# Sums of squares of queries and keys in the first attention: one matmul in full precision becomes two of parts

## The chip, the cores and the metric

The kernel runs on one core of a Trainium2 chip. The metric is the device time of one execution in microseconds (us). The core has TensorE (matmuls and the loads of their weights), VectorE, ScalarE and GpSimd, each with an instruction queue that it works through in order, and the queue that starts most transfers (SyncE).

## The reference

The kernel computes two transformer blocks one after the other, on 512 tokens of width 1024. The change lies in the first block's attention, which has 8 heads, each with two groups of 64 query and key columns:

```python
def rms_norm(x, g):
    xf = x.astype(jnp.float32)
    y = xf * lax.rsqrt(jnp.mean(xf * xf, axis=-1, keepdims=True) + EPS)
    return (y * g.astype(jnp.float32)).astype(x.dtype)

def diff_attention(q, k, v, q_norm_g, k_norm_g, ...):
    q = rms_norm(q, q_norm_g)
    k = rms_norm(k, k_norm_g)
    ...
        scores = jnp.einsum('bqhcd,bkhcd->bhcqk', q_blk, k).astype(jnp.float32) * scale
        scores = jnp.where(visible, scores, NEG_INF)
        probs = jax.nn.softmax(scores, axis=-1)
        diff = probs[:, :, 0] - lam * probs[:, :, 1]
```

What matters here is the mean of the squares of the 64 columns of each query and key. A second attention, an expert layer and two feed-forward layers follow; the change doesn't touch them.

## The kernel before

**Precision.** Most products are made of parts. An operand is split into a high part, a copy in the reduced 4-byte type (shown as fp32r), and a low part, the full value minus the high part, also stored in that type. `triple` (L719 to L721) issues three matmuls: high by high, high by low, low by high. ScalarE makes the high parts by `copy` (L1277), VectorE the low parts by `tt` with a subtraction (L1748). `linear` runs `triple` over k-steps of 128 rows: 8 k-steps of three matmuls are one projection to 128 columns for all 512 tokens. The sums of squares are different: one matmul of a constant matrix by the squares, both in plain 4-byte floats. The trace records such a matmul as two.

**Layout in the attention.** Features lie on the partitions and the 512 tokens on the columns. `bank[0]` to `bank[7]` are the eight banks of PSUM, where matmuls write. `qkf[i]` holds, for head h with i = h % 2, four buffers of 128 x 512: [0] and [1] for the query, [2] and [3] for the key; `qk[i]` is the same memory in the reduced type. In each pair the first is for the squares and later for the high part, the second for the raw values and later the scaled ones and the low part. `blk` is a constant 128 x 128 matrix with two blocks of ones, so that `blk` times the squares gives the sum over each group of 64, repeated on its partitions. `scr[6]` and `scr[7]` are the buffers for the roots of query and key.

**The order.** `attention_order` writes out one list of steps (235 of them), and every engine runs through the same list, doing its own part of each step. For a head from 2 to 6 the list from one query projection to the next scores of the head reads: q0 (k-steps 0 to 3 of the query projection), scores 4h-2, q1 (k-steps 4 to 7), qraw, turn 4h-3, weigh 4h-2, k0, scores 4h-1, k1, turn 4h-2, weigh 4h-1, v0, v1, vraw, scores 4h, oscale, turn 4h-1, weigh 4h, rows, scores 4h+1, g0, and so on. Each query block of a head is one step of scores, weigh (softmax and the difference of the two groups) and turn (transposing the weights through `tbank`). In short, by engine:

- TensorE. k1 (L845): waits for the square of the query, sums it into `bank[0]` (L846), then k-steps 4 to 7 of the key. v0 (L849): k-steps 0 and 1 of the value projection, waits for the square of the key, sums it into `bank[1]` (L854), then k-steps 2 to 4. v1: the sum of squares of the output of an earlier head into the same `bank[1]` (L862), which waits for the key's Ln to have read it, from head 2 on; then k-steps 5 to 7. Scores (L894, L896) of head h wait for the low part of its key. L908 are the transposes of turn.
- ScalarE. qraw: raw copy of the query out of `bank[0]`, then its square. k1: `root` of the query (Ln, then Exp, both at L1274), raw copy of the key, square. v0: a weight split, the query's high part, `root` of the key, the key's high part. Its other work between them: the exponentials of scores (two for each block), the high part of the turned weights (turn), and the high parts of weights (`whl<-raw`, 1024 columns).
- VectorE. k1: scales the query by the root (L1756). v0: low part of the query, scaling of the key, its low part. Its other work: the maxima of scores (L1913, L1914), weigh, the low part of the turned weights, and the low parts of weights.

A wait is an instruction on the engine that waits; what stands behind it in the queue waits as well. Weights are split four units ahead of their use. The constants land long before the attention.

Of the kernel before, what the change touches and what calls it, by code (L numbers as in the profile page):

```python
# [10 lines left out]
ALU = mybir.AluOpType  # L11
# [133 lines left out]
def f(ap):  # L145
    return ap.bitcast(F32)
# [345 lines left out]
def build(nc, a, out):  # L492
    with ExitStack() as ctx:
# [25 lines left out]
        scr_r, _ = at("scr_r", 10 * 512, F32R, offset=scr_off)  # L519
# [6 lines left out]
        rope_r, _ = at("rope_r", 1024, F32R, offset=rope_off)  # L526
# [7 lines left out]
        bank = [pb[:, 512 * i:512 * i + 512] for i in range(8)]  # L534
# [7 lines left out]
        def prm(name, i=0, n=1):  # L542
            return prm_t[:, PCOLS[name] + i:PCOLS[name] + i + n]

        ident, ones, blk, iota = cst(C_ID, 128), cst(C_ONE, 128), cst(C_BLK, 128), cst(C_IOTA, 128)
# [6 lines left out]
        Hh, Hl = cut(H_t, 8), cut(H_t[:, 4096:8192], 8)  # L552
# [19 lines left out]
        def wlo(j, o=0, n=None):  # L572
            return whi(j, 1024 + o, n or units[j][2])

        prod, act, dve, pool = signal("pe_products"), signal("act_results"), signal("dve_results"), signal("pool_results")
# [3 lines left out]
        cst_in, prm_in, lam_in = signal("constants_landed", 16), signal("parameters_landed", 16), signal("lambdas_landed", 16)  # L579
# [23 lines left out]
        qk = [cut(S_t[:, 8192 + 2048 * i:10240 + 2048 * i], 4) for i in range(2)]  # L603
        qkf = [cut(ST_t[:, 8192 + 2048 * i:10240 + 2048 * i], 4) for i in range(2)]
        vv = [cut(S_t[:, 12288 + 1024 * i:13312 + 1024 * i], 2) for i in range(2)]
        vvf = [cut(ST_t[:, 12288 + 1024 * i:13312 + 1024 * i], 2) for i in range(2)]
        dts = [cut(S_t[:, 14336 + 1024 * i:15360 + 1024 * i], 2) for i in range(2)]
        turned_hi = S_t[:, 14336:16000].rearrange("p (b q) -> p b q", b=13)
        turned_lo = (rope_r[:, 0:896].rearrange("p (b q) -> p b q", b=7),
                     S_t[:, 16000:16384].rearrange("p (b q) -> p b q", b=3))  # L610
        tbank, obank = bank[6], bank[7]
# [103 lines left out]
        def tensor(eng, e):  # L715
            q = Waits(eng, units)
# [6 lines left out]
            def linear(j, o, hh, hl, ready, done, ks=range(8), kk=8, n=T, start=True, stop=True):  # L723
                q.wait_ge(w_lo, j + 1)
                for k in ks:
                    q.wait_ge(dve, ready[k])
                    c = slice(128 * k, 128 * k + 128)
                    last = triple(o[:, 0:n], whi(j)[:, c], wlo(j)[:, c], hh[k], hl[k],
                                  start and k == 0, stop and k == kk - 1)
                if k == kk - 1:  # L730
                    last.then_inc(prod.up(("w", j), done), 1)
# [96 lines left out]
            def first_attention():  # L828
                for step in attention:
# [12 lines left out]
                        jk = q.unit("w_in", 8 + h)  # L842
                        linear(jk, bank[1], Hh, Hl, h1, None, range(4))
                    elif what == "k1":
                        q.wait_ge(act, ("q_sq", h))  # L845
                        e.matmul(bank[0], blk, qkf[h % 2][0], start=True, stop=True, skip_group_check=True).then_inc(  # L846
                            prod.up(("qs", h)), 1)
                        linear(jk, bank[1], Hh, Hl, h1, ("k", h), range(4, 8))
                    elif what == "v0":  # L849
                        jv = q.unit("w_in", 16 + h)  # L850
                        q.wait_ge(act, ("q_ln", h))
                        linear(jv, bank[0], Hh, Hl, h1, None, range(2))
                        q.wait_ge(act, ("k_sq", h))
                        e.matmul(bank[1], blk, qkf[h % 2][2], start=True, stop=True, skip_group_check=True).then_inc(  # L854
                            prod.up(("ks", h)), 1)
                        linear(jv, bank[0], Hh, Hl, h1, None, range(2, 5))
                    elif what == "v1":
                        before = ("k_ln", h)
                        for o in step[2]:
# [400 lines left out]
        def scalar(eng, e):  # L1260
# [11 lines left out]
            def run(func, o, x, own=False, **kw):  # L1272
                table(func, own)
                return e.activation(o, x, func, **kw)  # L1274

            def copy(o, x):
                return e.activation(o, x, ACT.Copy)  # L1277
# [127 lines left out]
            def first_attention():  # L1405
                for step in attention:
# [4 lines left out]
                    if what == "qraw":  # L1411
                        q.wait_ge(prod, ("q", h))
                        q.wait_ge(prod, ("scores", 4 * h - 5) if h > 1 else ("brr", 7))
                        copy(qkf[i][1], bank[0])
                        run(ACT.Square, qkf[i][0], bank[0]).then_inc(act.up(("q_sq", h)), 1)
                    elif what == "k1":
                        q.wait_ge(dve, ("q", h - 1) if h else ("m", 7))
                        root((("q_ln", h), ("q_r", h)), bank[0], scr[6], 64, ("qs", h))
                        q.wait_ge(prod, ("k", h))
                        copy(qkf[i][3], bank[1])  # L1420
                        run(ACT.Square, qkf[i][2], bank[1]).then_inc(act.up(("k_sq", h)), 1)
                    elif what == "v0":
                        q.wait_ge(dve, ("q_scaled", h))
                        copy(qk[i][0], qkf[i][1]).then_inc(act.up(("q_hi", h)), 1)
# [314 lines left out]
        def vector(eng, e):  # L1739
# [7 lines left out]
            def tt(o, x, y, op):  # L1747
                return e.tensor_tensor(o, x, y, op)  # L1748
# [6 lines left out]
            def stt(o, x, s, y, op0, op1, **kw):  # L1755
                return e.scalar_tensor_tensor(out=o, in0=x, scalar=s, in1=y, op0=op0, op1=op1, **kw)  # L1756
# [164 lines left out]
            def first_attention():  # L1921
                for step in attention:
                    what, h = step[0], step[1]
                    i = h % 2
                    if what in ("q0", "k0", "g0"):
                        weights("w_in", {"q0": 0, "k0": 8, "g0": 44}[what] + h)
                    if what == "k1":
                        q.wait_ge(act, ("q_r", h))
                        stt(qkf[i][1], qkf[i][1], prm("q_norm_g"), scr[6], ALU.mult, ALU.mult).then_inc(dve.up(("q_scaled", h)), 1)
                    elif what == "v0":  # L1930
                        q.wait_ge(act, ("q_hi", h))
                        tt(qk[i][1], qkf[i][1], f(qk[i][0]), ALU.subtract).then_inc(dve.up(("q", h)), 1)
# [847 lines left out]
```

## Time and profile before

| | |
|---|---|
| median of 3 runs | 2969.61 us (2969.41 to 2971.81) |
| profiled execution | 2972.36 us, span 2970.2 us |
| TensorE matmuls busy | 2921.5 us, 98% of the span |
| weight loads busy | 2509.6 us, 84% |
| VectorE busy | 1906.8 us, 64% |
| ScalarE busy | 1152.3 us, 39% |
| GpSimd busy | 842.9 us, 28% |
| chain that ended last | PE 80%, DVE 12%, ACT 4%, issue 3%, POOL 1% |
| first attention | about 250 to 527 us |

In the rows below PE is TensorE's matmuls, PEld its weight loads, DVE VectorE, ACT ScalarE. Matmuls are pipelined: one recorded with 0.39 us can have the next start 0.23 us after its own start. The duration of an instruction on DVE and ACT includes its latency; the next one on the same engine starts 0.06 to 0.13 us before that end if it doesn't need the result. The executed instruction's line is the helper's where a helper issues it (L1277 is every `copy`).

### The profile page before, as it was taken

What the parts mean: (1) busy time and instruction counts of PE and PEld (TensorE: products, weight loads), DVE (VectorE), ACT (ScalarE), POOL (GpSimd) and SP (SyncE); (2) the same over time, 40 slices, a digit from 0 to 9 for tenths busy, and PEclk for the clock granted to TensorE, in tenths of its full rate; (3) what the DMA queues carried; (4) which work ended last, traced back from release to release, by engine and by line L of the source; (5) the groups of instructions that cost most, each with busy time, mean ns of one, the idle gap of its engine ahead of it and who ended that gap; (6) DMA issues with size and microseconds to landing.
All of it is one profiled execution on the core that took longest, in us unless ns stands there. A gap on an engine that the chain in (4) does not pass through costs nothing.

```text
span 2970.2 us, 35823 instructions
## 1 busy us (share of the span) xinstructions
PE 2921.5 (98%) x14079; PEld 2509.6 (84%) x14079; DVE 1906.8 (64%) x3255; ACT 1152.3 (39%) x1704; POOL 842.9 (28%) x523
## 2 busy tenths in 40 slices
PE   8999999999999999999999999999999999999999
PEld 6877777789889999999999999998888877788887
DVE  6664665578888895426787788865444567644443
ACT  5674665443333334433323223223222355532221
POOL 0000000228788888872332232321000400210000
PEclk9999999999999999999999999999999999999999
DMA  4325564336656666798988888842332321133222
GB/s 141 112 92 212 199 223 167 132 103 144 136 127 139 153 154 146 166 272 322 333 311 308 287 310 314 318 142 86 99 100 94 122 71 50 51 99 99 93 93 71
DMA packets 240808, 489.29 MB, mean 165 GB/s; under 512 B 97664, under 2 KB 149440, under 8 KB 240128
## 3 DMA queue, kind: packets, MB, share of 16 engines
q1 hardware_dynamic: 175680, 417.87, 42.3%
q0 software_dynamic: 64960, 69.14, 10.3%
q8 instruction: 111, 1.82, 0.2%
q14 instruction: 57, 0.47, 0.0%
HBM read 443.18 MB, written 77.23 MB: 175 GB/s over the span
## 4 chain that ended last, share of the span: by engine, by line
PE 80%; DVE 12%; ACT 4%; issue 3%; POOL 1%; DMA 0%; SPq 0%; POOLq 0%; ACTq 0%
PE pb L719 25%; PE pb L721 25%; PE pb L720 25%; DVE whl L1748 2%; ACT scr L1274 2%; DVE ST L1748 1%; ACT whl L1277 1%; PE pb L1011 1%; DVE ST L1756 1%; DVE S L1748 1%; DVE su L1997 1%; DVE ST L1998 1%; DVE su L2000 1%; DVE scr L1748 1%; PE pb L894 1%
## 5 line engine op out<-in xcount | busy, mean ns | idle before, releaser
L719 PE MATMUL pb<-H,whl 128*128 128x512 f32 (+1 forms) x2400 | 939.7, 392 | 6.4 <-ACT scr L1274 2.3
L721 PE MATMUL pb<-H,whl 128*128 128x512 f32 (+1 forms) x2400 | 911.5, 380 | 0.0
L720 PE MATMUL pb<-H,whl 128*128 128x512 f32 (+1 forms) x2400 | 910.8, 380 | 0.0
L1748 DVE TENSOR_TENSOR whl<-raw,whl 128x1024 fp32r<-128x1024 f32 (+5 forms) x554 | 650.7, 1189 | 256.3 <-ACT whl L1277 219.8
L1277 ACT ACTIVATE whl<-raw 128x1024 fp32r<-128x1024 f32 (+5 forms) x554 | 544.6, 1003 | 361.2 <-PE pb L721 360.1
L719 PE MATMUL pb<-S,whl 128*128 128x448 f32 (+2 forms) x1732 | 654.9, 378 | 14.2 <-DVE S L1748 5.7
L720 PE MATMUL pb<-S,whl 128*128 128x448 f32 (+2 forms) x1732 | 649.6, 375 | 0.0
L721 PE MATMUL pb<-S,whl 128*128 128x448 f32 (+2 forms) x1732 | 649.5, 375 | 0.0
L719 PEld LDWEIGHTS pb<-H,whl 128*128 128x128 f32 x2400 | 451.4, 188 | 83.8 <-issue 8.8
L720 PEld LDWEIGHTS pb<-H,whl 128*128 128x128 f32 x2400 | 451.5, 188 | 72.2 <-issue 6.0
L721 PEld LDWEIGHTS pb<-H,whl 128*128 128x128 f32 x2400 | 450.6, 188 | 71.9
L2400 POOL DMA_INDIRECT gd<-scr,place x256 | 438.2, 1712 | 137.8 <-issue 77.1
L719 PEld LDWEIGHTS pb<-S,whl 128*128 128x128 f32 x1732 | 327.9, 189 | 60.9 <-DVE S L1748 7.2
L720 PEld LDWEIGHTS pb<-S,whl 128*128 128x128 f32 x1732 | 327.8, 189 | 42.6 <-issue 1.2
L721 PEld LDWEIGHTS pb<-S,whl 128*128 128x128 f32 x1732 | 327.6, 189 | 42.5
L2379 POOL TENSOR_TENSOR pad<-X 128x512 f32<-128x512 f32 x32 | 46.2, 1442 | 862.4 <-DVE X L1748 833.3
L1274 ACT ACTIVATE scr<-pb 128x448 f32<-128x448 f32 (+1 forms) x130 | 71.0, 546 | 386.2 <-PE pb L721 364.5
L1748 DVE TENSOR_TENSOR scr<-pb,scr 128x512 f32<-128x512 f32 x96 | 66.0, 691 | 210.7 <-PE pb L721 199.7
L2433 POOL DMA_INDIRECT scr<-in_pv_rows,su x64 | 94.8, 1482 | 232.1 <-DVE scr L1756 204.8
L1277 ACT ACTIVATE S<-GA 128x896 fp32r<-128x896 f32 x60 | 57.2, 953 | 252.6 <-DVE GA L1748 247.0
L2387 POOL DMA_INDIRECT scr<-in_pu_rows,su x64 | 91.8, 1434 | 217.0 <-DVE scr L1756 167.0
L1748 DVE TENSOR_TENSOR X<-X,pb 128x448 f32<-128x448 f32 (+1 forms) x144 | 86.2, 630 | 92.8 <-PE pb L721 78.8
(224 smaller groups left out, 2573.8 us busy)
## 6 DMA issues: line engine op xcount, KB each, us to landing
raw<-in_pu SPq DMA_DIRECT2D x128, 512.0 KB
raw<-in_pv SPq DMA_DIRECT2D x128, 512.0 KB
raw<-in_w_in SPq DMA_DIRECT2D x72, 512.0 KB
ad<-scr SPq DMA_DIRECT2D x128, 224.0 KB
GA<-gd SPq DMA_DIRECT2D x60, 448.0 KB, 4.2
GA<-ad SPq DMA_DIRECT2D x60, 448.0 KB, 5.9
raw<-in_wg SPq DMA_DIRECT2D x44, 512.0 KB
raw<-in_wu SPq DMA_DIRECT2D x44, 512.0 KB
```

Of the source, the lines that this page charges most:

```text
L719: e.matmul(o, lh, h, start=start, stop=False, skip_group_check=True)
L720: e.matmul(o, lh, l, start=False, stop=False, skip_group_check=True)
L721: return e.matmul(o, ll, h, start=False, stop=stop, skip_group_check=True)
L894: e.matmul(b[:, 0:keys], x[r, t], y[r, 0:keys], start=start, stop=False, skip_group_check=True)
L1011: last = e.matmul(bank[gbank[n % 4]][:, c], hot2[n % 4][:, c], hot1[n % 4][:, c], start=True, stop=True, skip_group_check=True)
L1274: return e.activation(o, x, func, **kw)
L1277: return e.activation(o, x, ACT.Copy)
L1748: return e.tensor_tensor(o, x, y, op)
L2379: e.tensor_tensor(one_sq if k else sum_sq, x, x, ALU.mult).then_inc(pool.up(), 1)
L2387: e.indirect_dma_start(urow[j % 3] if j < UROWS else tail_row[j % 4], None, a["pu_rows"], bass.IndirectOffsetOnAxis(ap=expert[:, j:j + 1], ...
L2400: e.indirect_dma_start(g_rows, bass.IndirectOffsetOnAxis(ap=place[:, b, h, k:k + 1], axis=0), TSv[:, b, h, k:k + 1], None, compute_op=ALU. ...
L2433: e.indirect_dma_start(tail_row[j % 4], None, a["pv_rows"], bass.IndirectOffsetOnAxis(ap=expert[:, j:j + 1], axis=0)).then_inc(row_in[j % ...
```

## The change

The matmul of `blk` with the squares becomes two, of `blk_r` with the high part and with the low part of the squares, into the same bank. `blk_r` is a copy of `blk` in the reduced type, made once by ScalarE in head 0, in a free part of `rope_r`. The high parts get buffers of their own, `sq_hi`, in the memory of `scr[6]` and `scr[7]`; the low parts go to `qk[i][0]` and `qk[i][2]`, over the squares. ScalarE's order in qraw and k1 is now: square, wait for it, high part, raw copy (before: raw copy, square). VectorE gets a subtraction in qraw, a step in which it had nothing to do, and one at the end of k1. TensorE waits in k1 and v0 for the raw copy and for the low part. In v0 the sum for the key stands behind three k-steps of the value projection, and two follow it (before: two and three).

```diff
+        blk_r, sq_hi = rope_r[:, 896:1024], [scr_r[:, 3072:3584], scr_r[:, 3584:4096]]
...
                     elif what == "k1":
-                        q.wait_ge(act, ("q_sq", h))
-                        e.matmul(bank[0], blk, qkf[h % 2][0], start=True, stop=True, skip_group_check=True).then_inc(
+                        q.wait_ge(act, ("q_raw", h))
+                        q.wait_ge(dve, ("q_sq_lo", h))
+                        e.matmul(bank[0], blk_r, sq_hi[0], start=True, stop=False, skip_group_check=True)
+                        e.matmul(bank[0], blk_r, qk[h % 2][0], start=False, stop=True, skip_group_check=True).then_inc(
                             prod.up(("qs", h)), 1)
                         linear(jk, bank[1], Hh, Hl, h1, ("k", h), range(4, 8))
                     elif what == "v0":
                         jv = q.unit("w_in", 16 + h)
                         q.wait_ge(act, ("q_ln", h))
-                        linear(jv, bank[0], Hh, Hl, h1, None, range(2))
-                        q.wait_ge(act, ("k_sq", h))
-                        e.matmul(bank[1], blk, qkf[h % 2][2], start=True, stop=True, skip_group_check=True).then_inc(
+                        linear(jv, bank[0], Hh, Hl, h1, None, range(3))
+                        q.wait_ge(act, ("k_raw", h))
+                        q.wait_ge(dve, ("k_sq_lo", h))
+                        e.matmul(bank[1], blk_r, sq_hi[1], start=True, stop=False, skip_group_check=True)
+                        e.matmul(bank[1], blk_r, qk[h % 2][2], start=False, stop=True, skip_group_check=True).then_inc(
                             prod.up(("ks", h)), 1)
-                        linear(jv, bank[0], Hh, Hl, h1, None, range(2, 5))
+                        linear(jv, bank[0], Hh, Hl, h1, None, range(3, 5))
...
                     if what == "qraw":
                         q.wait_ge(prod, ("q", h))
                         q.wait_ge(prod, ("scores", 4 * h - 5) if h > 1 else ("brr", 7))
-                        copy(qkf[i][1], bank[0])
                         run(ACT.Square, qkf[i][0], bank[0]).then_inc(act.up(("q_sq", h)), 1)
+                        if h == 0:
+                            q.wait_ge(cst_in, "cst")
+                            copy(blk_r, blk).then_inc(act.up("blk_r"), 1)
+                        q.wait_ge(act, ("q_sq", h))
+                        q.wait_ge(dve, ("q_scaled", h - 1) if h else ("m", 7))
+                        copy(sq_hi[0], qkf[i][0]).then_inc(act.up(("q_sq_hi", h)), 1)
+                        copy(qkf[i][1], bank[0]).then_inc(act.up(("q_raw", h)), 1)
                     elif what == "k1":
...
                         q.wait_ge(prod, ("k", h))
-                        copy(qkf[i][3], bank[1])
                         run(ACT.Square, qkf[i][2], bank[1]).then_inc(act.up(("k_sq", h)), 1)
+                        q.wait_ge(act, ("k_sq", h))
+                        if h:
+                            q.wait_ge(dve, ("k_scaled", h - 1))
+                        copy(sq_hi[1], qkf[i][2]).then_inc(act.up(("k_sq_hi", h)), 1)
+                        copy(qkf[i][3], bank[1]).then_inc(act.up(("k_raw", h)), 1)
...
-                    if what == "k1":
+                    if what == "qraw":
+                        q.wait_ge(act, ("q_sq_hi", h))
+                        tt(qk[i][0], qkf[i][0], f(sq_hi[0]), ALU.subtract).then_inc(dve.up(("q_sq_lo", h)), 1)
+                    elif what == "k1":
                         q.wait_ge(act, ("q_r", h))
                         stt(qkf[i][1], qkf[i][1], prm("q_norm_g"), scr[6], ALU.mult, ALU.mult).then_inc(dve.up(("q_scaled", h)), 1)
+                        q.wait_ge(act, ("k_sq_hi", h))
+                        tt(qk[i][2], qkf[i][2], f(sq_hi[1]), ALU.subtract).then_inc(dve.up(("k_sq_lo", h)), 1)
```

## Rows read from the trace of the kernel before

**Rows 1.** Busy time by stretch, one head: busy (x instructions), clock, DMA share.

```profile
394.00:426.00 32.00, 32.00 (x163) 24.09 (x164) 20.10 (x46) 19.63 (x43) 0.00 (x0) 1.00 0.56 206
```

**Rows 2.** Waits of the weight loads, 255 to 495 us: in total, times, longest.

```profile
PEld pb L854 <- ACT ST L1274: 3.1, 8, 0.4
PEld pb L894 <- DVE S L1748: 0.8, 2, 0.5
```

**Rows 3.** Order of time, TensorE, head 5: start, duration, engine, line, operation.

```profile
414.17 1.10 PE L846 MATMUL pb<-ST,cst 128*128 128x512 f32 x2
...
415.34 0.39 PE L720 MATMUL pb<-H,whl 128*128 128x512 f32 x1
...
419.43 0.39 PE L721 MATMUL pb<-H,whl 128*128 128x512 f32 x1
419.81 1.12 PE L854 MATMUL pb<-ST,cst 128*128 128x512 f32 x2
...
421.00 0.40 PE L720 MATMUL pb<-H,whl 128*128 128x512 f32 x1
...
422.84 1.02 PE L862 MATMUL pb<-ST,cst 128*128 128x512 f32 x2
...
423.93 0.40 PE L720 MATMUL pb<-H,whl 128*128 128x512 f32 x1
...
425.88 0.55 PE L894 MATMUL pb<-S 64*128 64x128 f32 x6
```

**Rows 4.** Order of time, ScalarE, head 5; idle time before in brackets.

```profile
410.33 0.60 ACT L1277 ACTIVATE ST<-pb 128x512 f32<-128x512 f32 x1 [0.34 <-PE pb L721]
410.82 0.59 ACT L1274 ACTIVATE ST<-pb 128x512 f32<-128x512 f32 x1
411.30 0.39 ACT L1277 ACTIVATE S<-pb 128x256 fp32r<-128x256 f32 x1
...
417.44 0.68 ACT L1274 ACTIVATE scr<-pb,cst 128x512 f32<-128x512 f32 x1
418.15 0.63 ACT L1274 ACTIVATE scr<-scr 128x512 f32<-128x512 f32 x1
...
419.17 0.59 ACT L1274 ACTIVATE ST<-pb 128x512 f32<-128x512 f32 x1
419.64 0.49 ACT L1277 ACTIVATE S<-pb 128x384 fp32r<-128x384 f32 x1
...
420.96 0.64 ACT L1277 ACTIVATE S<-ST 128x512 fp32r<-128x512 f32 x1
421.48 0.70 ACT L1274 ACTIVATE scr<-pb,cst 128x512 f32<-128x512 f32 x1
```

**Rows 5.** Order of time, VectorE, head 5.

```profile
411.72 0.42 DVE L1748 TENSOR_TENSOR rope_r<-pb,S 128x256 fp32r<-128x256 f32 x1 [3.00 <-ACT S L1277]
...
414.58 0.68 DVE L1913 TENSOR_REDUCE sm<-pb 128x1 f32<-128x512 f32 x1
...
422.29 0.68 DVE L1748 TENSOR_TENSOR S<-ST,S 128x512 fp32r<-128x512 f32 x1
...
424.33 0.69 DVE L1748 TENSOR_TENSOR S<-ST,S 128x512 fp32r<-128x512 f32 x1 [0.70 <-ACT S L1277]
```

**Rows 6.** Order of time, heads 0 and 1, VectorE, TensorE, weight loads.

```profile
268.08 0.69 DVE L1748 TENSOR_TENSOR S<-ST,S 128x512 fp32r<-128x512 f32 x1 [0.70 <-ACT S L1277]
...
269.10 0.55 PE L894 MATMUL pb<-S 64*128 64x128 f32 x6
...
298.15 0.41 PEld L894 LDWEIGHTS pb<-S 64*128 64x128 f32 x6 [0.47 <-DVE S L1748]
```

**Rows 7.** Order of time, TensorE, end of the stage.

```profile
527.82 0.51 PE L719 MATMUL pb<-S,whl 128*128 128x512 f32 x1 [1.53 <-DVE S L1748]
...
531.94 0.51 PE L719 MATMUL pb<-S,whl 128*128 128x512 f32 x1 [1.78 <-DVE scr L1748]
```

**Rows 8.** Busy time by stretch there: the clock is the last but two.

```profile
530.00:540.00 10.00, 8.21 (x29) 6.53 (x29) 6.74 (x9) 4.41 (x7) 0.00 (x0) 0.83 0.46 156
```

## The prediction

> **What bounds the kernel now.** I read the page first: TensorE is busy 98% of the span, so what it does without waiting is on the path. Then the busy time by stretch: in the 32 us of one head of the first attention TensorE is busy for all 32.00 us at a granted clock of 1.00, VectorE for 20.10 and ScalarE for 19.63 [rows 1]. So removed TensorE time counts in full here, and the other two engines have room on average. The average isn't enough, because all three engines follow one written-out order. The third view is the list of waits of the weight loads from 255 to 495 us: the key sum of squares, L854, waits for ScalarE in every head, 8 times of 0.4 us at most, 3.1 us in all, and the score matmuls L894 wait twice for the key's low part [rows 2]. Of each 0.4 us TensorE itself loses only 0.15 (419.43 + 0.23 = 419.66 to 419.81), since a prefetched load stands ahead of its matmul [rows 3]. Small as that is, it says that L854 has no slack. So the fourth view is the order of time of head 5, engine by engine [rows 3 to 5]; heads 2 to 7 have these rows six times, 31.9 us apart; one set stands for them. The reader is to find there what L854 waits for and how far back that chain goes without a gap.
>
> **The chain before L854.** ScalarE gets the query projection at 410.33, copies and squares it, and at 411.30 makes the high part of the turned weights [rows 4]. VectorE, idle for 3.00 us, starts on that at 411.72 and is then busy without a gap: low part, weighing, a weight split, the maxima of scores 19 at 414.58 [rows 5]. The scores themselves end at about 414.35 (L846 follows them at 414.17 while they drain) [rows 3], so the maxima wait for VectorE by 0.2 us. ScalarE's exponentials wait for the maxima, and behind them stand, in its order, the Ln and Exp of the query root (417.44, 418.15), copy and square of the key (the square at 419.17) [rows 4]; L854 starts at 419.81, 0.05 after the square ends at 419.76 [rows 3]. From 410.33 to 419.81 this is a chain of ScalarE and VectorE work; whatever is put into it comes out at L854.
>
> **What is removed.** A sum of squares in full precision is two recorded matmuls that hold TensorE for four passes. After L862, which nothing holds up, the next L720 starts at 423.93; one pass of 0.23 earlier is the end of the sum: 423.70 - 422.84 = 0.86. After L846 it is 415.34 - 0.23 - 414.17 = 0.94, after the waiting L854 421.00 - 0.23 - 419.81 = 0.96: a weight load that isn't prefetched shows with 0.10 [rows 3]. No row has a pass with the block matrix in the reduced type; the nearest are the passes of the projections, 0.23 apart with a new weight load each. I take 0.46 for two, 0.56 behind a wait. Bounds: nothing gained (0.94) and 0.46. So L846 gives back 0.38 us a head, and L854 with its wait (419.43 + 0.23 = 419.66 to 420.77, 1.11 us) up to 0.65.
>
> **What the query side adds.** The square comes first, then a copy to its high part, which waits for the finished square, then the raw copy. The wait costs 0.59 + 0.03 (the Exp starts 0.03 after the end of the Ln, 417.44 + 0.68 to 418.15) where the square's successor came after 0.48: 0.14. The added copy, SBUF to SBUF, has a pace of 0.52 (420.96 to 421.48) [rows 4]. Together 0.66. VectorE's new subtraction has the form of the one at 422.29, 0.68 us [rows 5]; it waits for the high part (411.58) and ends at 412.30. L846 at 414.17 is covered: 1.9 us of slack. But the high part of the turned weights moves from 411.30 to 411.96 and VectorE's next start from 411.72 to 412.38, and from there the chain has no gap: maxima 415.24, Ln 418.10, Exp 418.81. Queued behind VectorE's new wait are the turned weights, weighing and the split; none of these has a tight reader on TensorE but the maxima. I bound this shift by 0 (absorbed) and 0.80 (the copy at 0.63 in full); I take 0.66.
>
> **What the key side adds.** The same edit once more. Square 419.35 to 419.94; high part 419.97 to 420.60; VectorE's low part, behind the query scaling, which is done by 420.2, 420.63 to 421.31; TensorE 421.36 instead of 419.81. TensorE itself arrives at 419.66 - 0.38 + 3 x 0.23 (the third k-step now stands ahead) = 419.97, so it idles for 1.39 us: the moved step covers 0.69 of 2.1 us. It is not lost work, for it is then missing behind: two k-steps instead of three. Behind the key's square ScalarE is late by 2 x 0.66 = 1.32: turned weights 420.96, query high part 422.28, Ln of the key 422.80 to 423.50 [rows 4].
>
> **What is late next.** L862, the sum for the head output before, overwrites the bank that this Ln reads and waits for it. Before, the Ln ended at 422.18 and L862 started at 422.84: 0.66 of slack. Now TensorE arrives at 421.36 + 0.56 + 6 x 0.23 = 423.30 and the Ln ends at 423.50, so L862 starts at 423.55, with 0.10 for its load: +0.81 against 422.84. The passes up to L894 (425.88) are unchanged. The key's low part starts at 424.33 [rows 5]; 1.32 later it ends at 426.34, before L894 starts at 426.69. After L894 all three engines are late by the same 0.81, so the next head starts the same chain over: 0.81 x 6 for heads 2 to 7 = 4.9 us. The price of the passes drops out, since ScalarE sets the time.
>
> **Heads 0 and 1.** Head 1 has no L862, and its scores already wait for the key's low part (the weight loader idles 0.47 before 298.15) [rows 6]; the whole 1.32 shows: 1.3 us. In head 0 there are no weights to turn and no maxima, so only the key side counts: square after the key product, which TensorE now ends 0.40 earlier, two copies and the wait: the Ln comes 0.3 later, the key's low part ends at 269.05 instead of 268.77, and L894 stands at 269.10 [rows 6]: 0.0. The copy of the block matrix (128 columns) lies in ScalarE's idle time there. Bounds for head 0: -0.9 (both gains) to +0.3.
>
> **Sum.** 0 + 1.3 + 4.9 = 6.2 us more. The scores of head 7 carry it, and the chain to the end of the stage runs on from them through VectorE and ScalarE, so it is kept. The profiled execution took 2972.36 us (span 2970.2), 2.75 above the median of 2969.61. Against its own time: 2978.6; as a median 2975.8, or +0.21%. A measurement of this kernel tells about 0.2%, 5.9 us, from no change.
>
> **Rivals.** (A) The chain isn't as tight as I read it and the third k-step covers the key side: then L846 gives 0.38 and L854 0.65 in 8 heads, -8.2 us, 2961.4. It needs the key's parts within 0.16 us of where the square now ends (419.97 against 419.81); against it stand three operations in a row that take 1.9 us. It decides from 1.39 us: a chain shorter by that much leaves no stall. (B) The query side's shift is absorbed, as VectorE's 3.00 us of idle time before 411.72 suggests; against it, that idle time lies before, not behind. Then only 0.66 reaches the Ln: L862 at 422.89 plus the load, +0.15 x 6, and 0.66 in head 1: +1.6, 2971.2. (C) The clock. At 527.82 TensorE resumes after 1.53 us of idle time at full pace; at 531.94 it resumes after 1.78 more [rows 7], and in the stretch from 530 to 540 the granted clock is 0.83 on average, where it was 1.00 before [rows 8]: 0.17 x 10 us / 0.5 = 3.4 us at 1.2 instead of 2.4 GHz, 1.7 us of work lost. With a stall of 1.39 and one of 0.25 in each of seven heads, 7 x 1.7 on top: +18.1, 2987.7. For it speaks the likeness, against it that the second gap is small. The Trainium skill, "TensorE: Matmul & The Clock Gate", section "HAM oscillation — how this bites in real kernels", says that waits between bursts of matmuls bring the slow clock back; the trace agrees at 531.94 and doesn't at 527.82.
>
> **How the numbers follow.** Forecast 0.75, A 0.07, B 0.14, C 0.04. The forecast's own range has 0.5 to 1.1 us a head in heads 2 to 7 and 1.0 to 1.6 in head 1: +4.0 to +8.2, 2973.6 to 2977.8; the border of 5.9 us lies in its middle, so 0.41 of it is slower and 0.34 the same. With B and some room above: 2970.4 to 2979.5. Slower 0.41 + 0.04, the same 0.34 + 0.14, faster 0.07.
>
> **What would show it.** Right: L854 with an idle time of about 1.4 us behind VectorE in heads 1 to 7; the maxima of the last score block of a head 0.66 later against L846; L862 behind the key's Ln; heads 32.7 us apart instead of 31.9. Wrong: L854 follows the third k-step at once (A); the Ln of the query root isn't later against L846 (B); passes of 0.43 us inside the stage (C).

## The result, and the profile after

| | before | after |
|---|---|---|
| median | 2970.63 us (2969.41 to 2971.81, 9 runs) | 2976.66 us (2974.59 to 2983.99, 9 runs) |
| profiled execution | 2972.36 us, span 2970.2 | 2976.09 us, span 2974.3 |

The ratio is 1.0021, with a 95% interval of 1.0013 to 1.0029: 6.0 us slower in the median, and the interval reaches from 3.9 to 8.6 us. The forecast was 6.2 us.

The page: TensorE has 5.2 us less to do (2921.5 us before), and the span is longer all the same.

```profile
span 2974.3 us, 35872 instructions
...
PE 2916.3 (98%) x14079; PEld 2510.0 (84%) x14079; DVE 1917.4 (64%) x3271; ACT 1162.1 (39%) x1721; POOL 844.0 (28%) x523
```

The stretch of head 6 (the columns are those of [rows 1], where TensorE was busy for all 32.00 us). Now it is idle for 32.00 - 30.87 = 1.13 us, with its clock unchanged; VectorE has 0.55 us more in the same 32 us and ScalarE 0.42:

```profile
426.00:458.00 32.00, 30.87 (x159) 23.32 (x158) 20.65 (x45) 20.05 (x45) 0.00 (x0) 1.00 0.56 206
```

What the weight loads waited for from 255 to 500 us (in total, times, longest), against [rows 2]. The wait of the key's sum, here L858, has grown from 3.1 to 5.3 us; new are waits of L720, the value projection, for the query's Ln and of L867, the sum for the head before, for the key's Ln; the scores L899 wait in all eight heads. In heads 2 to 7 that is 0.35 us each and only the load that nothing prefetches: the scores start 0.33 us after the last pass of the value projection before (425.55 to 425.88) and 0.32 after (430.04 to 430.36). Heads 0 and 1 wait for the key's low part, 0.83 and 1.23 us:

```profile
PEld pb L720 <- ACT scr L1279: 7.7, 7, 1.1
...
PEld pb L858 <- ACT ST L1282: 5.3, 8, 0.7
...
PEld pb L899 <- DVE S L1763: 4.2, 8, 1.2
PEld pb L867 <- ACT scr L1279: 2.6, 6, 0.4
```

Head 5 in order of time, TensorE, against [rows 3] (L848 and L849 are the query's two passes, L858 and L859 the key's, L867 was L862, L899 was L894, L913, the transposes, was L908):

```profile
417.85 0.48 PE L848 MATMUL pb<-scr_r,rope_r 128*128 128x512 f32 x1
...
418.40 0.40 PE L720 MATMUL pb<-H,whl 128*128 128x512 f32 x1
...
421.16 0.49 PE L913 MATMUL pb<-cst,scr 128*128 128x128 f32 x3
422.50 0.50 PE L720 MATMUL pb<-H,whl 128*128 128x512 f32 x1 [0.85 <-ACT scr L1279]
...
425.14 0.47 PE L858 MATMUL pb<-scr_r,rope_r 128*128 128x512 f32 x1 [0.28 <-ACT S L1282]
...
425.69 0.39 PE L720 MATMUL pb<-H,whl 128*128 128x512 f32 x1
...
427.23 1.12 PE L867 MATMUL pb<-ST,cst 128*128 128x512 f32 x2
...
430.36 0.55 PE L899 MATMUL pb<-S 64*128 64x128 f32 x6
```

ScalarE, against [rows 4] (the square is L1279, copies are L1282):

```profile
414.00 0.60 ACT L1279 ACTIVATE ST<-pb 128x512 f32<-128x512 f32 x1 [0.34 <-PE pb L722]
414.63 0.63 ACT L1282 ACTIVATE scr_r<-ST 128x512 fp32r<-128x512 f32 x1
415.17 0.58 ACT L1282 ACTIVATE ST<-pb 128x512 f32<-128x512 f32 x1
415.64 0.38 ACT L1282 ACTIVATE S<-pb 128x256 fp32r<-128x256 f32 x1
...
421.76 0.68 ACT L1279 ACTIVATE scr<-pb,cst 128x512 f32<-128x512 f32 x1
...
423.02 0.58 ACT L1279 ACTIVATE ST<-pb 128x512 f32<-128x512 f32 x1
423.63 0.63 ACT L1282 ACTIVATE scr_r<-ST 128x512 fp32r<-128x512 f32 x1
424.17 0.58 ACT L1282 ACTIVATE ST<-pb 128x512 f32<-128x512 f32 x1
424.64 0.48 ACT L1282 ACTIVATE S<-pb 128x384 fp32r<-128x384 f32 x1
...
426.48 0.69 ACT L1279 ACTIVATE scr<-pb,cst 128x512 f32<-128x512 f32 x1
```

VectorE, against [rows 5] (L1763 at 415.29 and 424.30 are the two new low parts, at 416.05 the turned weights', L1928 the first of the maxima, 429.32 the key's low part):

```profile
415.29 0.69 DVE L1763 TENSOR_TENSOR S<-ST,scr_r 128x512 fp32r<-128x512 f32 x1 [2.90 <-ACT scr_r L1282]
416.05 0.42 DVE L1763 TENSOR_TENSOR rope_r<-pb,S 128x256 fp32r<-128x256 f32 x1
...
418.91 0.68 DVE L1928 TENSOR_REDUCE sm<-pb 128x1 f32<-128x512 f32 x1
...
424.30 0.69 DVE L1763 TENSOR_TENSOR S<-ST,scr_r 128x512 fp32r<-128x512 f32 x1 [0.40 <-ACT scr_r L1282]
...
429.32 0.69 DVE L1763 TENSOR_TENSOR S<-ST,S 128x512 fp32r<-128x512 f32 x1 [0.70 <-ACT S L1282]
```

The profile names ScalarE for the idle time ahead of L858. Of the two things that L858 waits for, the raw copy ended at 424.17 + 0.58 = 424.75 and VectorE's low part at 424.30 + 0.69 = 424.99, so the low part is the later.

The positions are best read from the start of the query's sum in each head:

| from the query's sum, heads 2 to 7 | before | forecast | after |
|---|---|---|---|
| maxima of the last scores start | 0.41 | 1.07 | 1.06 |
| key's sum starts | 5.64 | 7.19 | 7.29 |
| sum for the head before starts | 8.67 | 9.38 | 9.38 |
| scores start | 11.70 | 12.52 | 12.51 |
| (head 1) scores start | 10.92 | 12.24 | 12.23 |

From the start of head 0's sum of the query to score block 28 the kernel before takes 230.77 us, the changed one 236.69. The 5.92 us between them are the effect but for 0.08: from score block 28 to the last sum of squares of the stage it takes 33.43 us before and 33.51 after. I call the first distance the stage's and use it below, because it repeats to 0.02 us (236.67 in another execution), while the time of a whole execution varies by several us.

### The profile page after: what moved, and what is told of

The parts are those of the page before. It is cut to its first block, busy times and chain, and to the rows that moved or that the text cites. A ratio compares the mean times of both kernels' runs of the same rounds, so it can differ in the third digit from the quotient of the medians.

```text
span 2974.3 us, 35872 instructions
## 1 busy us (share of the span) xinstructions
PE 2916.3 (98%) x14079; PEld 2510.0 (84%) x14079; DVE 1917.4 (64%) x3271; ACT 1162.1 (39%) x1721; POOL 844.0 (28%) x523
## 4 chain that ended last, share of the span: by engine, by line
PE 78%; DVE 13%; ACT 6%; issue 2%; POOL 1%; DMA 0%; SPq 0%; POOLq 0%; ACTq 0%
PE pb L720 25%; PE pb L722 25%; PE pb L721 25%; DVE whl L1763 2%; ACT scr L1279 2%; ACT whl L1282 1%; DVE S L1763 1%; PE pb L1016 1%; DVE su L2017 1%; DVE ST L2018 1%; DVE su L2020 1%; DVE ST L1763 1%; DVE ST L1771 1%; DVE scr L1771 1%; DVE scr L1763 1%
## 5 line engine op out<-in xcount | busy, mean ns | idle before, releaser
L720 PE MATMUL pb<-H,whl 128*128 128x512 f32 (+1 forms) x2400 | 933.5, 389 | 12.2 <-ACT scr L1279 8.0
L1763 DVE TENSOR_TENSOR whl<-raw,whl 128x1024 fp32r<-128x1024 f32 (+5 forms) x554 | 650.4, 1188 | 247.2 <-ACT whl L1282 242.2
L1282 ACT ACTIVATE whl<-raw 128x1024 fp32r<-128x1024 f32 (+5 forms) x554 | 544.8, 1003 | 357.9 <-PE pb L722 356.7
L720 PE MATMUL pb<-S,whl 128*128 128x448 f32 (+2 forms) x1732 | 654.2, 378 | 15.6 <-DVE whl L1763 5.8
L720 PEld LDWEIGHTS pb<-H,whl 128*128 128x128 f32 x2400 | 451.9, 188 | 87.4 <-ACT scr L1279 11.2
L720 PEld LDWEIGHTS pb<-S,whl 128*128 128x128 f32 x1732 | 327.4, 189 | 62.5 <-DVE S L1763 7.1
L1279 ACT ACTIVATE scr<-pb 128x448 f32<-128x448 f32 (+1 forms) x130 | 70.9, 545 | 379.0 <-PE pb L722 350.8
L1763 DVE TENSOR_TENSOR scr<-pb,scr 128x512 f32<-128x512 f32 x96 | 66.0, 690 | 210.1 <-PE pb L722 199.1
L1282 ACT ACTIVATE S<-GA 128x896 fp32r<-128x896 f32 x60 | 57.2, 953 | 255.5 <-DVE GA L1763 255.5
L1763 DVE TENSOR_TENSOR X<-X,pb 128x448 f32<-128x448 f32 (+1 forms) x144 | 86.2, 629 | 89.0 <-PE pb L722 73.8
```

Source lines behind the costliest of these rows:

```text
L720: e.matmul(o, lh, h, start=start, stop=False, skip_group_check=True)
```

## The experiments

The distances are those of one execution each (those of a head are medians over heads 2 to 7). The ratio compares the times of 8 to 11 executions with those of the kernel before on the same chip, with a 95% interval.

| run | maxima | key's sum | head before's sum | scores | head 1 scores | stage | ratio of the times |
|---|---|---|---|---|---|---|---|
| before | 0.41 | 5.64 | 8.67 | 11.70 | 10.92 | 230.77 | |
| changed, again (e8) | 1.06 | 7.29 | 9.38 | 12.52 | 12.23 | 236.67 | 1.0019 (1.0009 to 1.0028) |
| e1 query alone | 1.06 | 6.30 | 9.34 | 12.38 | 11.57 | 235.04 | 1.0024 (1.0015 to 1.0034) |
| e2 key alone | 0.41 | 6.64 | 8.74 | 11.88 | 11.58 | 232.62 | 1.0009 (1.0000 to 1.0019) |
| e3 two k-steps ahead | 1.06 | 7.29 | 9.90 | 12.95 | 12.22 | 239.62 | 1.0030 (1.0019 to 1.0040) |
| e4 one split moved | 0.20 | 6.44 | 8.53 | 11.65 | 11.38 | 230.81 | 1.0005 (0.9995 to 1.0014) |
| e5 both splits moved | 0.20 | 6.44 | 8.37 | 11.38 | 11.36 | 233.43 | 1.0007 (0.9998 to 1.0016) |
| e6 before, splits moved | 0.20 | 5.44 | 8.46 | 11.50 | 10.70 | 229.88 | 0.9998 (0.9988 to 1.0007) |
| e7 key ahead of root | 0.20 | 5.98 | 7.83 | 11.51 | 11.51 | 234.96 | 1.0033 (1.0020 to 1.0047) |
| e9 reordered | 0.20 | 5.98 | 7.82 | 10.86 | 10.67 | 225.40 | 0.9991 (0.9982 to 1.0000) |
| e10 before, splits in idle time | 0.20 | 5.45 | 8.49 | 11.53 | 10.72 | 229.50 | 0.9998 (0.9989 to 1.0007) |
| e11 before, one copy more | 0.89 | 6.12 | 9.16 | 12.20 | 11.41 | 234.20 | 1.0013 (1.0004 to 1.0022) |

**Query alone, key alone (e1, e2).** The change taken apart. For the key, e1 goes back on ScalarE to the lines marked + here, and on TensorE and VectorE to those of the kernel before (left out); e2 does the same for the query:

```diff
-                        run(ACT.Square, qkf[i][2], bank[1]).then_inc(act.up(("k_sq", h)), 1)
-                        q.wait_ge(act, ("k_sq", h))
-                        if h:
-                            q.wait_ge(dve, ("k_scaled", h - 1))
-                        copy(sq_hi[1], qkf[i][2]).then_inc(act.up(("k_sq_hi", h)), 1)
-                        copy(qkf[i][3], bank[1]).then_inc(act.up(("k_raw", h)), 1)
+                        copy(qkf[i][3], bank[1])
+                        run(ACT.Square, qkf[i][2], bank[1]).then_inc(act.up(("k_sq", h)), 1)
...
```

> The change for the query alone, the key as in the kernel before. All offsets are from the start of the query's sum in head 5 (before: L846 at 414.17; L854 5.64 later, L862 8.67, L894 11.71). Theory (a chain from the query projection through turned weights, maxima, exponentials and roots sets the time): the chain is 0.66 us longer, so the key's sum comes at 6.30, L862 at 9.33, the scores at 12.37, although the query's sum holds TensorE 0.38 us less. 0.66 in each of heads 1 to 7, about -0.3 in head 0: score block 28 starts 4.3 us later than before, the time rises by about 4.3 us. Rival 1 (the passes are what counts and the chain has slack): -0.38 in each head, -3.0 us. Rival 2 (the loss comes from the key side alone): 0.

> The change for the key alone, the query as in the kernel before. Theory: the key's sum comes 6.52 after the start of the query's (before 5.64), the next head's sum L862 waits for the key's Ln (0.66 later, against 0.66 of slack) and comes at 8.82 (before 8.67), the scores 0.15 later; head 1, whose scores wait for the key's low part, 0.66, head 0 0.25: score block 28 starts 1.8 us later than before, the time rises by about 1.8 us. With the query alone this adds up to the 6.1 us of the whole change. Rival 1 (the key side carries the loss): 5 to 6 us. Rival 2 (passes count): -0.40 a head plus the wait of 0.15, -4.4 us.

Measured: 4.27 and 1.85 us more in the stage, 6.12 together against 5.92 for both. The larger loss comes from the half whose own sum was covered: the query's sum lost nothing at its own place, its extra ScalarE work came out at the key's sum 6 us later. The key's half is nearly absorbed by the 0.66 us of slack of the sum for the head before (8.74 against 8.67).

**One copy more (e11).** The chain by itself, without any pass changed:

```diff
                     if what == "qraw":
...
+                        q.wait_ge(dve, ("q_scaled", h - 1) if h else ("m", 7))
+                        copy(scr_r[:, 3072:3584], bank[0])
                         copy(qkf[i][1], bank[0])
```

> The kernel before the change with one copy more on ScalarE in qraw, out of the query's bank into memory that nobody reads, ahead of the raw copy. Theory: the copy has a pace of 0.49 us and all of it comes out at the key's sum, which TensorE has no slack for: 6.13 after the query's (5.64), the sum for the head before 9.16, the scores 12.19; 0.49 in heads 1 to 7, nothing in head 0: 3.4 us more, score block 28 234.2 us after head 0's sum of the query. Rival (ScalarE is busy 61% of this stage and hides it): 0.

3.43 us in the stage, 0.49 in each of seven heads, and the maxima are late by 0.48 already. A copy that nobody reads, on an engine that is idle for 12 of 32 us, costs its whole pace. It shows the chain of the prediction by itself.

**The moved k-step (e3).**

> The changed kernel with the key's sum behind two k-steps of the value projection, as before, in place of three. Theory: the sum starts at the same time (the parts come no earlier, TensorE idles 0.69 us more), and one more k-step stands behind it, so that L867 is no longer held by the key's Ln but by TensorE: 0.44 us later in heads 2 to 7, nothing in head 1, 0.15 in head 0: score block 28 2.8 us later than in the changed kernel, the time 2.8 us longer. Rival (the key's Ln alone holds it, so the moved k-step is worth nothing): 0.

The key's sum stays at 7.29 and what follows comes 0.52 later, the scores 0.44; the stage takes 2.93 us more than the changed kernel's. So the k-step in front was worth 2.9 us: it fills a stall, and without it L867 is bound by TensorE again.

**The split ahead of the maxima (e4).**

```diff
-                    if what in ("q0", "k0", "g0"):
-                        weights("w_in", {"q0": 0, "k0": 8, "g0": 44}[what] + h)
+                    if what in ("q0", "k1", "g0"):
+                        weights("w_in", {"q0": 0, "k1": 8, "g0": 44}[what] + h)
```

> The changed kernel with VectorE's split of a weight unit in step k0 (1.14 us, ahead of the last maxima of a head) moved to step k1, behind them. Theory: the maxima start when their scores are there, 0.2 after the query's sum starts instead of 1.06; all behind them comes 0.86 earlier: the key's sum at 6.43 instead of 7.29, L867 at 8.5 instead of 9.38, the scores at 11.64 instead of 12.51. 0.87 in each of heads 1 to 7: 6.1 us less than the changed kernel, so about the time of the kernel before. Rival 1 (the chain doesn't run through the maxima but from the k-product or from ScalarE's copies alone): 0. Rival 2 (the weight's low part now comes too late, or its buffer too late for the load): slower, with waits of the projections for VectorE.

VectorE in head 5 of this run; its query's sum starts at 415.23 and the maxima 0.20 later, now behind TensorE and not behind VectorE:

```profile
415.43 0.69 DVE L1928 TENSOR_REDUCE sm<-pb 128x1 f32<-128x512 f32 x1 [0.19 <-PE pb L901]
```

Everything after it is 0.86 earlier, the stage takes 230.81 us, 5.88 less than the changed kernel's: the loss is gone, by a move of one split that touches neither a square nor a pass. That kernel is then as fast as the one before, not faster.

**Both splits (e5), and the same two moves in the kernel before (e6).** ScalarE's split of v0 goes behind the key's high part:

```diff
...
                         copy(qk[i][2], qkf[i][3]).then_inc(act.up(("k_hi", h)), 1)
+                        weights("w_in", 16 + h)
...
```

> The run before this with one more move: ScalarE's high part of a weight unit in step v0 (0.95 us, ahead of the query's high part and the key's Ln) goes behind the key's high part. Offsets from the start of the query's sum, in heads 2 to 7. Theory: the key's sum stays at 6.44; the key's Ln comes 0.95 earlier and no longer holds the sum for the head before, which TensorE reaches at 8.38 (8.53), the scores come at 11.42 (11.65; in the kernel before the change 11.70). In head 1 the scores come at 10.55 (11.38), when TensorE is there. About 2.1 us less than the kernel before the change, 8 less than the changed kernel. Rival (the key's Ln doesn't hold that sum any more once the maxima are early): 8.53 and 11.65 as they were, the gain only in head 1, 0.8 us.

> The kernel before the change, full precision in one pass of its own, with the same two weight splits moved. Theory: the maxima start 0.2 earlier, so the key's sum is ready at 5.44 and TensorE, which reaches it at 5.49 (5.64), is the bound; the sum for the head before at 8.42 (8.67), the scores at 11.46 (11.70); 0.24 in heads 2 to 7, 0.3 in head 1: about 1.8 us less than the kernel before. The chain then has no more to give, and what two passes save can be read against this run. Rival (the moved splits alone are worth the 6 us that they took off the changed kernel): 6 us less than the kernel before.

In heads 2 to 7 the scores come at 11.38 as expected; in head 1 they come at 11.36, not at 10.55, where they still wait for the key's low part (the loader is idle for 1.21 us). And the stage is 2.62 us longer than e4's, not 2.1 shorter than the kernel before: this expectation failed above all behind the scores, where I had not looked. The transposes of the value's rows, L875, now wait for the raw value, 5.9 us in six heads (TensorE is idle for 0.74 in head 5). In e6 the same happens on a smaller scale (1.3 us at L870; 0.9 us gained in the stage, 1.8 expected). e6 also answers its rival: the moves that took 6 us off the changed kernel have little to take off the one before, since TensorE is the bound there after 0.2 us.

**The key's squares ahead of the root (e7).** ScalarE's order in k1, with e5's splits; v0 has its copy and root in the like order, and VectorE makes the low part of the key's squares ahead of the query's scaling:

```diff
-                        root((("q_ln", h), ("q_r", h)), bank[0], scr[6], 64, ("qs", h))
+                        q.wait_ge(prod, ("qs", h))
+                        run(ACT.Ln, scr[6], bank[0], scale=1.0 / 64, bias=eps).then_inc(act.up(("q_ln", h)), 1)
                         q.wait_ge(prod, ("k", h))
...
                         copy(qkf[i][3], bank[1]).then_inc(act.up(("k_raw", h)), 1)
+                        run(ACT.Exp, scr[6], scr[6], scale=-0.5).then_inc(act.up(("q_r", h)), 1)
```

> The changed kernel with both splits moved and ScalarE's order in k1 and v0 changed: Ln of the query, square, high part and raw copy of the key, then Exp of the query root; Ln of the key, then the query's high part, then Exp of the key's. VectorE makes the low part of the key's squares ahead of the query's scaling. Theory: the key's parts are ready at 5.78, when TensorE is still at the third k-step (5.92): no idle time of note is left, and the 0.38 and 0.40 us of the passes show. The sum for the head before at 7.76, the scores at 10.80 (before the change 11.70, with moved splits 11.46); in head 1 10.6 (10.92). 0.9 in heads 2 to 7, 0.3 each in heads 0 and 1: 6.1 us less than the kernel before, 4.3 less than that kernel with moved splits. Rival 1 (the passes in the reduced type save nothing of their own): as the kernel before with moved splits. Rival 2 (a later wait takes over, above all that of the scores for the key's low part): scores later than 11.2 at a key's sum of 5.9.

The first half came out (5.98, 7.83), the second is its rival 2: scores at 11.51, and the stage is 4.2 us longer than that of the kernel before, where 6.1 less were expected. The waits of the weight loads from 255 to 495 us (total, times, longest), then head 5 of this run on TensorE, ScalarE and VectorE:

```profile
PEld pb L899 <- DVE S L1769: 9.0, 8, 1.9
...
PEld pb L875 <- ACT ST L1282: 5.0, 5, 1.0
```

```profile
429.15 0.55 PE L899 MATMUL pb<-S 64*128 64x128 f32 x6 [0.57 <-DVE S L1769]
...
431.09 0.66 PE L875 MATMUL pb<-cst,ST 128*128 128x128 f32 x4 [0.76 <-ACT ST L1282]
```

```profile
427.74 0.63 ACT L1282 ACTIVATE S<-ST 128x512 fp32r<-128x512 f32 x1 [1.73 <-DVE ST L1777]
428.28 1.04 ACT L1282 ACTIVATE whl<-raw 128x1024 fp32r<-128x1024 f32 x1
...
430.46 0.58 ACT L1282 ACTIVATE ST<-pb 128x512 f32<-128x512 f32 x1
```

```profile
425.69 0.75 DVE L1777 SCALAR_TENSOR_TENSOR scr<-scr,sm 128x512 f32<-128x512 f32 x1
426.36 0.68 DVE L1769 TENSOR_TENSOR S<-ST,S 128x512 fp32r<-128x512 f32 x1
426.96 0.74 DVE L1777 SCALAR_TENSOR_TENSOR ST<-ST,prm,scr 128x512 f32<-128x512 f32 x1
```

Two waits have taken over. VectorE weighs the last scores (425.69) and makes the query's low part (426.36) before it comes to the key's scaling (426.96); the scores wait 0.57 us for what follows from that. And ScalarE's split, moved to 428.28, now stands ahead of the raw value (430.46), for which the transposes L875 wait 0.76 us, as in e5.

**Reordered (e9), and its control (e10).** On top of e7, the split of v0 goes to where both engines are idle (on VectorE ahead of that of g0), and the last weighing of a head to k1:

```diff
                         copy(vv[i][0], bank[0]).then_inc(act.up(("v_hi", h)), 1)
+                        weights("w_in", 16 + h)
...
                     elif what == "k1":
+                        if h:
+                            weigh(4 * h - 1)
                         q.wait_ge(act, ("k_sq_hi", h))
```

> The changed kernel with the order of the run e7, and two of its faults mended: the weight split of step v0 goes into idle time (ScalarE behind the value's high part in rows, VectorE ahead of the split in g0) instead of ahead of the raw value, and VectorE weighs the last scores of a head in k1, where it is idle for 2.1 us, instead of between the query's and the key's parts. Theory (the second chain, key's Ln to key's low part, holds the scores of e7, and the raw value holds rows): the key's sum at 5.98 after the query's, the sum for the head before at 7.83, the scores at 10.87 in heads 2 to 7 (e7: 11.51, before the change 11.70), no wait of the transposes L875. Score block 28 starts 225.6 us after head 0's sum of the query (before the change 230.8, changed 236.7): 5.2 us less than the kernel before. Rival 1 (another wait takes over): scores at 11.3 or later, or a distance between heads over 31.4. Rival 2 (the time outside this stage grows by what the stage gives back): the distance as said, the time as before.

> The kernel before the change (one full-precision matmul) with the three weight splits where e9 has them and nothing else. Theory: the key's sum at 5.44, the sum for the head before at 8.46, the scores at 11.50, as in the run e6, but without the wait of the transposes: score block 28 229.2 us after head 0's sum of the query, 1.5 us less than the kernel before. What e9 has beyond it is what two passes save once no chain holds TensorE. Rival (the moved splits are worth as much here as in the changed kernel): 5 us less or more.

e9 does in the stage what was expected (225.40 against 225.6): 31.08 us from head to head, 5.37 us less than the kernel before. From 255 to 495 us, the scores' wait is 0.37 us in heads 2 to 7, a load without prefetch; in heads 0 and 1 it is 1.08 us, so there the key's low part still holds them:

```profile
PEld pb L899 <- DVE S L1769: 4.4, 8, 1.1
...
PEld pb L720 <- ACT scr L1279: 1.7, 7, 0.2
...
PEld pb L858 <- ACT ST L1282: 0.5, 1, 0.5
```

e10 is the kernel before with the three splits where e9 has them and nothing else changed; it gains 1.27 (1.5 expected). The 4.1 us between them lie in heads 2 to 7, 0.67 in each, and not in heads 0 and 1 (0.02 and 0.08). What they consist of can be read from head 5, first in e10, then in e9:

```profile
412.65 1.10 PE L846 MATMUL pb<-ST,cst 128*128 128x512 f32 x2
...
413.82 0.39 PE L720 MATMUL pb<-H,whl 128*128 128x512 f32 x1
...
418.10 1.12 PE L854 MATMUL pb<-ST,cst 128*128 128x512 f32 x2
...
419.29 0.39 PE L720 MATMUL pb<-H,whl 128*128 128x512 f32 x1
```

```profile
412.10 0.48 PE L848 MATMUL pb<-scr_r,rope_r 128*128 128x512 f32 x1
...
412.65 0.40 PE L720 MATMUL pb<-H,whl 128*128 128x512 f32 x1
...
418.08 0.39 PE L858 MATMUL pb<-scr_r,rope_r 128*128 128x512 f32 x1
...
418.54 0.40 PE L720 MATMUL pb<-H,whl 128*128 128x512 f32 x1
```

With a pass of 0.23 us taken off as in the prediction, the query's sum holds TensorE for 0.94 us in e10 and 0.55 in e9, the key's for 0.96 and 0.46: 0.89 us of TensorE time saved a head. Of this 0.23 goes back ahead of the value projection, which starts 0.48 us after the transposes before it in e9 (415.42 to 415.90) and 0.25 in e10 (416.36 to 416.61), waiting for the query's Ln. The difference, 0.66, is what is seen. So the 4.1 us are the passes; e9's order doesn't add to them but lets them show.

In time e9 takes 2968.74 us against 2971.89 for the kernel before on that chip, but the interval of the ratio ends at 1.0000, so the gain in time is only just told from nothing, and 3.15 us is less than the 5.4 of the stage. Against the changed kernel (1.0021 and 1.0019) e9's 0.9991 is faster.

**The changed kernel again (e8)**, for the size of its own effect:

> The changed kernel itself, on the same chip as the three others, since the times of different calls differ by a few us. Theory: the offsets of its own trace again (7.29, 9.38, 12.51), score block 28 5.9 us later against the start of head 0's sum than in the kernel before; 5.9 us more than the kernel before in the time. Rival (the 3.7 us by which the profiled executions differ are the true difference): 3.7 us.

The stage takes 236.67 us again, 1.0019 in time. The 3.7 us between the two profiled executions are not the effect: from the end of the last sum of squares of the stage (L930 in the changed kernel) to the first matmul of another kind at about 1092 us the same code took 566.1 us in the profile of after, 568.7 in this one and 568.1 in the kernel before.

## Why the prediction was right, point by point

**The chain.** Right, and it carried the forecast: the maxima 0.65 late against L846 (forecast 0.66), shown by e11 (a dose of 0.49 in gives 0.49 out) and e4 (0.86 taken out gives 0.86 back).

**What is removed.** The two passes take 0.55 us (417.85 to 418.40, 425.14 to 425.69), not 0.46 as taken for the query's: a weight load shows there in both. It didn't matter, since TensorE was not the bound. Where a sum waits for nothing, as the key's in e9, its two passes do take 0.46.

**The query side.** Right. The added copy and the wait move the low part of the turned weights from 2.45 us ahead of the query's sum (411.72 against 414.17) to 1.80 ahead (416.05 against 417.85): 0.65 us, 0.66 forecast. The new subtraction at 415.29 fits into VectorE's idle time. The bound of 0, that the idle time of 3.00 us absorbs it (rival B), is ruled out by e1.

**The key side.** The size was right to 0.1 us: 7.29 against 7.19. The place of the stall was not. I put 1.39 us of idle time ahead of the key's sum. In fact v0 opens with a wait for the query's Ln, which reads the bank that the value projection overwrites; before, that Ln ended at 417.44 + 0.68 = 418.12 [rows 4] and the first pass of the value projection started 0.05 later, without slack, and I passed over it:

```profile
417.88 0.49 PE L908 MATMUL pb<-cst,scr 128*128 128x128 f32 x3
418.17 0.50 PE L719 MATMUL pb<-H,whl 128*128 128x512 f32 x1
```

So TensorE now idles 0.85 us there and 0.28 ahead of L858. Counted from start to start, as the prediction does, the value projection starts 1.34 us after the transposes L913 (421.16 to 422.50; before 0.29 after L908), 1.05 more, and L858 0.46 later than the pass of 0.23 before it would allow (424.45 + 0.23 = 424.68, against 425.14): 1.51 us in two places against 1.39 in one. Both waits are for the same chain, and it sets when the key's sum starts however the idle time ahead of it is divided; that is why the forecast didn't suffer.

**What is late next.** Right: the key's Ln ends at 426.48 + 0.69 = 427.17, L867 starts at 427.23, 9.38 after the query's sum. e3 shows the other side of it: with one k-step less in front, TensorE is the bound.

**Heads 0 and 1.** In head 1 the scores' wait for the key's low part carries the whole 1.31 us, in head 0 nothing is lost: from the query's sum to the scores it takes 10.08 us, 10.12 before. From there to head 1's query sum it is 17.94 us, 18.13 before, because the transposes L875 no longer come after the scores with a gap of 0.27 us but of 0.07; I had no term for this.

**Rivals.** A is refuted by e1 and e2, neither of which is faster. B needed an Ln of the query's root that doesn't move; it starts 3.91 us after the query's sum (421.76 against 417.85), 3.27 before (417.44 against 414.17 [rows 3, 4]). C didn't occur: the granted clock is 1.00 in the stage with stalls of 0.85 and 0.28 us.

**The sum.** 6.2 forecast, 5.92 in the stage, 6.0 in the medians. By heads, from the query's sum to the scores: -0.04 in head 0 (0 forecast), 1.31 in head 1 (1.3), and in heads 2 to 7 12.51 - 11.70 = 0.81 by the table, 0.78 to 0.85 one by one (0.81). These add up to 6.1; head 0's -0.19 behind its scores makes the 5.9. The error of 0.1 us in the two passes dropped out. The nearness of 6.0 in the medians to 6.2 proves little by itself, since the interval reaches from 3.9 to 8.6; the distances in the stage are what confirms the terms.

## What to carry to other kernels

Where three engines walk one written-out order, look past the busy shares for the wait without slack and follow it back to the last idle time; whatever is added between the two is paid in full, even if the instruction it serves is covered by microseconds. Removing work from the engine that is busy 98% of the time pays nothing while such a chain holds it; shortening the chain (here one weight split of 1.14 us moved behind the maxima) pays at once, until TensorE itself is the bound, and only then does the removed work show. And a split or a copy moved out of one chain lands in front of something: name what stands behind its new place before moving it.

## What the runs showed of the hardware

TensorE's clock took part of e9's gain. Behind the stage both kernels have two idle times of 1.53 and 1.78 us. In the kernel before the clock falls there (0.83 from 530 to 540 us [rows 8]), the slow passes end up under the next wait, 1.94 us at 567.75, and the clock is 1.00 afterwards:

```profile
567.75 0.50 PE L719 MATMUL pb<-S,whl 128*128 128x512 f32 x1 [1.94 <-DVE S L1748]
```

```profile
567.00:572.00 5.00, 4.25 (x19) 3.52 (x20) 1.95 (x3) 2.87 (x3) 0.00 (x0) 1.00 0.77 251
```

In e9, 5 us ahead, the same idle times leave the clock at 1.00; TensorE therefore reaches the next wait 1.6 us sooner, idles 3.51 us, and the clock falls behind it (0.69 on average from 562 to 567 us, the level of 1.2 GHz for part of it), where nothing hides the slow passes:

```profile
524.90:534.90 10.00, 8.23 (x36) 6.67 (x36) 6.74 (x9) 4.42 (x7) 0.00 (x0) 1.00 0.46 159
562.00:567.00 5.00, 4.35 (x13) 3.46 (x14) 1.87 (x3) 2.77 (x3) 0.00 (x0) 0.69 0.72 248
```

```profile
562.65 0.50 PE L720 MATMUL pb<-S,whl 128*128 128x512 f32 x1 [3.51 <-DVE S L1769]
```

The wait ends at the same distance from the last sum of squares of the stage in both (44.57 us), and e9 is 5.10 us ahead there (562.65 against 567.75); about 1.6 us of them are lost behind it. The stall of 3.5 us and the slow passes behind it appear in e1, e3 and e7 as well; in both executions of the changed kernel and in all the others the clock falls behind the second of the two gaps and the stall is 1.9 to 2.0 us. Those four are also the ones in which the code after the stage took longest: 569.2 to 570.5 us, against 566.1 to 568.8 in the nine others. What decides in which gap the clock falls these runs don't show; that a change elsewhere can move it, and that this is worth 1.6 us either way, they do. The rest of the spread, and most of the difference between e7's 4.2 us in the stage and 9.1 in the medians (2985.10 against 2975.98), stays unexplained. It is the reason to measure such a change by the stage and not by the time alone.
